# Each weight slot loaded by two 512 KB DMAs from one queue in place of one 1 MB DMA

## What is computed

```python
# first_block: two layers on x and, in the first of them, on a context
mod = (silu_c @ ada_w[i] + ada_b[i])[:, None, :]          # 1024 -> 6 x 1024, for both layers
h = modulate(rmsnorm(x, norm_mix_w[i]), sh_m, sc_m)
y, y_c = ab_mixer(...) if i % 2 == 0 else cd_mixer(...)   # gated MLP + neighbourhood attention; Fourier + linear attention
x = x + g_m * y
x = x + g_f * swiglu(modulate(rmsnorm(x, norm_ffn_w[i]), sh_f, sc_f), w_gate, w_up, w_down)
...
# second_block: two layers, each mixer -> layer_norm -> cross_attention -> layer_norm -> feed-forward -> layer_norm
mix = even_mixer(...) if i % 2 == 0 else odd_mixer(...)
ff = dense_swiglu(...) if i % 2 == 0 else moe_swiglu(...) # 8 experts of hidden width 3584, top 2
```

## Time and profile before

| | |
|---|---|
| median of 3 runs | 3240.34 us (3239.83 to 3241.69) |
| profiled execution | 3230.18 us |
| its span | 3228.4 us, mean granted TensorE clock 0.918 |
| PE busy | 2952.9 us, 91% of the span |
| DVE, ACT busy | 1857.8 us (58%), 1178.0 us (36%) |
| moved by DMA | 596.59 MB, mean 185 GB/s |

### The profile page before, as it was taken

The page is one execution under the profiler, slowest core; times in us unless marked ns, Lnnn a source line. Parts: engine busy times, 40 slices in busy tenths (PEclk is TensorE's granted clock), DMA queues, the critical chain, the costliest instruction groups (busy, mean ns, idle before and its releaser), DMA issues.

```text
span 3228.4 us, 38045 instructions
## 1 busy us (share of the span) xinstructions
PE 2952.9 (91%) x14218; PEld 2273.9 (70%) x14218; DVE 1857.8 (58%) x2618; ACT 1178.0 (36%) x1671; POOL 7.0 (0%) x15
## 2 busy tenths in 40 slices
PE   4798989999877999688999999979999999999998
PEld 0333548888646998566898755758888888888886
DVE  0102545545335774533786366248888788888887
ACT  1211410000231001232101233137777777777776
POOL 0000000000000000000000000000000000000000
PEclk7898999999987999779999855889999999999999
DMA  9543012223212553112454300218898898898986
GB/s 410 208 165 135 15 64 95 100 91 103 80 39 88 194 179 142 40 49 95 139 175 142 131 1 1 105 52 314 333 374 333 325 374 332 346 360 332 373 326 232
DMA packets 82665, 596.59 MB, mean 185 GB/s; under 512 B 9040, under 2 KB 10064, under 8 KB 11024
## 3 DMA queue, kind: packets, MB, share of 16 engines
q1 hardware_dynamic: 80960, 583.04, 47.9%
q0 software_dynamic: 1616, 12.32, 0.9%
HBM read 594.28 MB, written 1.05 MB: 184 GB/s over the span
## 4 chain that ended last, share of the span: by engine, by line
PE 86%; DVE 6%; DMA 3%; ACT 2%; issue 2%; ACTq 0%; SPq 0%; DVEq 0%; POOLq 0%
PE bank L435 14%; PE bank L605 8%; PE bank L609 7%; PE bank L608 7%; PE bank L1319 6%; PE bank L1322 6%; PE bank L1323 6%; PE bank L449 4%; PE bank L744 4%; PE bank L731 3%; PE bank L1352 3%; PE bank L1355 3%; PE bank L1356 3%; DMA ring<-in_stream 2%; PE bank L737 2%
## 5 line engine op out<-in xcount | busy, mean ns | idle before, releaser
L575 DVE TENSOR_TENSOR ring_part<-ring,arena_part 128x2048 fp32r<-128x2048 f32 x437 | 984.0, 2286 | 59.5 <-ACT arena_part L1588 54.9
L1588 ACT ACTIVATE arena_part<-ring 128x2048 fp32r<-128x2048 f32 x339 | 642.5, 1918 | 153.6 <-DMA ring<-in_stream 153.5
L605 PE MATMUL bank<-arena_part 128*128 128x256 f32 (+1 forms) x1584 | 509.7, 322 | 30.7 <-issue 24.4
L609 PE MATMUL bank<-arena_part,ring_part 128*128 128x256 f32 (+1 forms) x1584 | 506.0, 319 | 0.0
L1319 PE MATMUL bank<-arena_part 128*128 128x512 f32 x896 | 354.9, 396 | 3.1 <-issue 2.7
L1322 PE MATMUL bank<-ring_part,arena_part 128*128 128x512 f32 x896 | 349.8, 390 | 0.0
L1323 PE MATMUL bank<-arena_part 128*128 128x512 f32 x896 | 349.4, 390 | 0.0
L605 PEld LDWEIGHTS bank<-arena_part 128*128 128x128 f32 x1584 | 303.2, 191 | 59.6 <-issue 26.0
L608 PE MATMUL bank<-h_part,arena_part 128*128 128x256 f32 (+1 forms) x1056 | 338.2, 320 | 0.0
L435 PE MATMUL bank<-h_normed,ring 128*128 128x256 f32 (+1 forms) x1024 | 312.4, 469 | 25.4 <-issue 11.6
L609 PEld LDWEIGHTS bank<-arena_part,ring_part 128*128 128x128 f32 x1584 | 303.5, 192 | 20.9
(11 more groups left out here) (250 smaller groups left out, 3572.7 us busy)
## 6 DMA issues: line engine op xcount, KB each, us to landing
ring<-in_stream SPq DMA_DIRECT2D x555, 1024.0 KB, 4.8
consts<-in_small POOLq DMA_DIRECT2D x1, 3067.0 KB, 14.5
arena<-in_ab_bias POOLq DMA_DIRECT2D x1, 2048.0 KB, 34.1
arena<-in_t_bias POOLq DMA_DIRECT2D x1, 2048.0 KB, 9.8
x_stream<-in_x_t POOLq DMA_DIRECT2D x1, 1024.0 KB, 21.2
x_stream<-in_ctx_t POOLq DMA_DIRECT2D x1, 1024.0 KB, 27.6
x_stream<-in_mem_t POOLq DMA_DIRECT2D x1, 1024.0 KB, 5.8
arena<-in_band_bias POOLq DMA_DIRECT2D x1, 1024.0 KB, 11.7
```

The source lines that it names most:

```text
L575: return nc.vector.tensor_tensor(low, value, high.bitcast(F32), ALU.subtract)
L605: m = nc.tensor.matmul(out_ap, w_high, high, start=start, stop=False)
L609: return nc.tensor.matmul(out_ap, w_low, high, start=False, stop=stop)
L1588: nc.scalar.activation(high, ring[:, where], ACT.Copy).then_inc(sem("moe_high"), 1)
```

## The change

Line 2137 issued one DMA for a slot. Now a loop over two parts issues two, both from SP's queue, each of 1024 columns (4096 bytes in each partition, 512 KB): first the left half of the slot, then the right. Both raise the same semaphore of the slot by 16, so it gains 32 for each slot, and all who wait for a landing wait for multiples of 32: for both halves. The wait for `slots_used` stands ahead of the first half alone.

```diff
             def landed(self):
                 n = self.t // TILES
-                v = 16 * (n // RING + 1)
+                v = 32 * (n // RING + 1)
                 if self.i is not None:
-                    v = v + self.i * (16 * self.per // RING)
+                    v = v + self.i * (32 * self.per // RING)
                 self.book.eng.wait_ge(sem(f"slot_landed{n % RING}"), v)
...
-            landed = 16 * (n // RING + 1)
-            book.eng.wait_ge(sem(f"slot_landed{n % RING}"), landed if i is None else landed + i * (16 * per // RING))
+            landed = 32 * (n // RING + 1)
+            book.eng.wait_ge(sem(f"slot_landed{n % RING}"), landed if i is None else landed + i * (32 * per // RING))
...
-                            16 * v if i is None else 16 * v + i * (16 * SLOTS_EXPERT // RING))
+                            32 * v if i is None else 32 * v + i * (32 * SLOTS_EXPERT // RING))
...
                 at = n if at is None else at
-                sp.dma_start(ring[:, n % RING * SLOT:(n % RING + 1) * SLOT], stream[at, :, :])\
-                    .then_inc(sem(f"slot_landed{n % RING}"), 16)
+                for part in range(2):
+                    cols = slice(part * SLOT // 2, (part + 1) * SLOT // 2)
+                    first = n % RING * SLOT
+                    sp.dma_start(ring[:, first + cols.start:first + cols.stop], stream[at, :, cols])\
+                        .then_inc(sem(f"slot_landed{n % RING}"), 16)
```

## The result

| | median | lowest to highest | ratio to before |
|---|---|---|---|
| before | 3240.09 us | 3237.9 to 3241.69, 4 runs | |
| after | 3256.51 us | 3253.45 to 3260.59, 4 runs | 1.0052, 95% interval 1.0035 to 1.0069 |
| after, run a second time among the experiments | 3258.02 us | 3246.51 to 3272.28, 10 runs | 1.0067, 1.0043 to 1.0090 |

The change makes the kernel slower by 16.4 us; the ratio's interval allows 11.3 to 22.4 us. The forecast was +3.1 us, and its range ended at 3252.5. So the forecast time was wrong, and so was its statement that the change stays within 0.2%.

A forecast was written before the change was run, and what follows sets the result against it. PE was taken to bound the kernel, with loads limiting only the ada products. 38 slots at 0.081 us gave +3.1 us, SP's issues and the experts nothing: 3240.34 + 3.1 = 3243.4 us, range 3238.5 to 3252.5.

The forecast's parts named there:

- What bounds the kernel: Whole kernel: PE busy 91% of the span; transfers limit only the ada products; experts' DMA share 0.89, PE waits short.
- Parts 1 and 2: Ring loads: 4 KB packets add 72 ns, the second semaphore packet 9 ns; a DMA-limited slot goes from 2.49 to 2.57 us.
- How many slots pay: Ada products: 24 slots through the third group and 14 in the next three, 38 at 0.081 us, +3.1 us.
- The sum for ada: Ada products: total forecast loss of +3.1 us, with bounds of -0.1 and 12.2 us.
- Part 3: SP's queue: the second issue adds some 0.46 us per slot, hidden behind the first half's transfer; cost nothing.
- Part 4: Experts: landing moves from 4.8 to about 4.9 us, ACT's idle time takes up 0.1 us; cost nothing.
- The cover: Experts: ACT's idle time before line 1621, 50.5 us in 47 waits, 1.1 us each, was to absorb later landings.
- A pause at each DMA: Rival, ada and experts: each added DMA costs 0.24 us on the DMA engines; 3252.5 to 3259 us; chance 0.12.
- The serial fixed cost: Rival, all loads: 2.3 us fixed cost paid for each DMA, 7.2 us per slot, 4640 us total; chance 0.01.
- the faster phase: Rival, earlier stages: a shifted start changes time at the lower clock; up to 8 us faster, 3235 us; chance 0.04.

The follow-up runs named there:

- Experiment 2: One DMA per slot as in the kernel before, but the slot lies in HBM as two contiguous halves, giving 256 rows of 4 KB without gaps; 3225.06 us, ratio 0.9991.
- Experiment 3: The changed kernel with its two DMAs per slot, but each half laid out in HBM as one contiguous 512 KB block; 3239.98 us, ratio 1.0016.
- experiment 8: Kernel before's one DMA per slot, but with 4 KB rows, each followed in HBM by 4 KB not read; 3245.29 us, ratio 1.0021.
- experiment 12: The kernel before, unchanged, run and traced again as a control; 3235.07 us, ratio 0.9999.
- experiment 9: Kernel before's one DMA per slot, but with rows of 4 KB every 4608 bytes in HBM, 512 bytes left out between; 3227.73 us, ratio 0.9988.

## Why the prediction was wrong

**What bounds the kernel** was read rightly for the ada products: the same pieces are in the chain, and their number did not change. For the experts it was read from PE's eight short waits and the DMA share of 0.89, and those say only that nothing was late before, not by how little.

**Parts 1 and 2, the price of packets: right.** 2.57 us per slot was forecast; the second group shows 2.57 and 2.55, the fourth 2.54 behind a first step of 2.89. Experiment 2, which has the packets and not the rest, lost 3.4 us in ada against 3.1.

**How many slots pay: the right count of the wrong thing.** 38 slots at 0.081 us give what the cadence costs. But a burst also has a beginning, and there the fourth group lost 2.1 us before its first landing. "The ring's queue has the DMA engines without a pause in these stretches" is still true after (92.4% against 94.4%); only they moved 1.59 MB in place of 2.34. The sum for ada was mis-sized: it measured 9.8 us, and the missing term is 9.8 - 3.1 = 6.7 us. Experiments 3 and 8 each reach into it: without the gaps 3.2 us are given back, and with the gaps but one DMA the whole loss is there, 10.8 us. The two causes therefore don't simply add, and how they share the 6.7 us is open.

**Part 3, "Cost: nothing": doubtful.** That SP "can hand over a DMA in less than half the time" holds for the median issue, 333 ns. But it was read from six DMAs, which may not have filled the queue: with twice as many at the start, SP's eleventh and twelfth issue took 3.94 and 3.35 us. And in the first burst of a group single issues stood for much longer, as SP's line of the kernel after from 138.6 to 152 us shows (ns min/median/max):

```profile
L2140 SPq DMA_DIRECT2D ring<-in_stream x14: 332/333/1143, 138.7 to 151.3; - x14
...
DMA to landing us min/median/max: 4.7/9.1/11.1
```

1143 ns is nearly the 1.28 us that a half takes to move. Experiment 3, with contiguous halves, has such an issue as well (1303 ns) and lost 3.2 us more in ada than experiment 2; that the long issues cost this was not tested. After the first 12 us the kernel after has 14 issues over 600 ns, before has one. 11 of the 14 start within 1.5 us behind an instruction fetch in the trace, and only 28 of the 1084 shorter ones do; that the fetch is the cause was not tested either.

**Part 4, the experts: the step that failed.** "A landing comes 4.8 us after its issue and moves to about 4.9 us" had the size from packets alone. It moved to 6.8 us. The prediction had named the stretch of the experts growing by more than a few us as its sign that ACT's idle time did not cover a landing, and that is what came: 10.8 us. The cover was named and sized rightly, 1.1 us at a time; 2.0 us of lateness go through it, and L1621's 50.5 us fell to 0.3. The sentence "if the cover were gone each slot would pay its 0.08 us" was also wrong in kind. What is paid is not a rate per slot but a wait of up to 1.5 us at the start of an expert, where ACT's chain has too little slack, and the clock behind it. PE's waits at L1286 account for 9.8 - 4.6 = 5.2 us. The lower clock accounts for roughly 10.3 us x 0.47 = 4.8, an estimate: at the third expert PE became 4.1 us later, of which the longer wait is 0.9, and the other 3.2 go with 6.8 us at the lower level. Together this is 10.0 of the 10.8 us. The rest I cannot name.

**The rivals.** "A pause at each DMA" had a chance of 0.12, and its 3252.5 to 3259 holds the measured time, but by luck, not by its mechanism. It priced a constant 0.24 us per DMA, with the experts bound by DMA from 0.22 us on. There is no such constant: experiment 3 has all the DMAs and lost 0.3 us in the experts. What did happen is the sentence beside it, that a half "read from HBM with gaps of 4 KB between its rows could have the same effect". That was known from the diff and had no row of before for or against it, since every transfer there is contiguous. An unknown that no row bounds should have carried a rival of its own, and widened the range to 3260 or so. The serial fixed cost (4640 us) and the faster phase did not occur. The scatter by the clock is real, and larger than the 8 us allowed for it: within the attention alone experiment 12 shows 12.9 us between two executions of before.

**The sum.** By trace the change costs 9.8 + 10.8 = 20.6 us, and 24.3 the second time. The runs say 16.4 us (11.3 to 22.4) the first time. The second time the medians lie 16.0 us apart, and the ratio gives 21.7 us (13.9 to 29.2; 0.0067, 0.0043 and 0.0090 of 3242). The difference is within what the clock moves from run to run.

**Settled**, as far as one profile of each kernel can, is that rows of 4 KB at 8 KB distance make landings late, in one DMA or two, that late landings cost time in the experts, and that neither 4 KB packets nor the number of DMAs does so there. **Open** is why the distance of 8 KB is slow where 4608 bytes are not, why the start of a burst in ada is slow, and what holds single issues of SP for a microsecond.

No variant beats before beyond the measurement: experiments 2 and 9 have ratios of 0.9991 and 0.9988, both with 1 inside their intervals.

## What to carry to other kernels

Cutting a DMA by columns changes three things: the size of its packets, the number of issues, and the distance between the rows that one DMA reads. The first could be priced from rows of before, the second only in part; for the third, lay the data out so that each piece stays contiguous, or take the price as unknown. Where loads run just ahead of their use, the DMA share says little; compare the change in landing time (the last of the 16 engines, not the mean) with the consumer's idle time at that point, and when the change is larger, expect waits at the place with the least slack. To compare two executions whose clock differs, line them up by the same instruction and read each stage by itself.

## What the hardware did that was not expected

- DMAs over 64 partitions moved 220 GB/s with 8 KB packets of about 600 ns; over 128 partitions 310 ns each. The kernel took 22% longer.
- Rows of 4 KB read at 8 KB distance: the median packet is as fast as ever (159 ns), but the last of 16 engines is 1.5 to 1.8 us behind the first, against 0.4 without gaps in one DMA and 0.95 in contiguous halves. At a distance of 4608 bytes it was 0.7.
- Rows of 8 KB at 16 KB distance also landed late, 5.8 us in place of 4.8 (spread 1.6), and yet the back-to-back loads of the ada groups lost only 1.1 us.
- An issue of 333 ns took up to 1.6 us now and then, and 3.9 us at the start behind ten others; a DMA whose pattern has one dimension more took 373 ns to issue (experiments 2, 8 and 9).
- Two executions of one program differ by 12.9 us in 100 us of attention, with PE's clock at its lower level for 10.2 us in one and 44.4 in the other.
